# Expert sort ahead of the first row tables, and those tables behind the first half of the first expert products

## The reference

```python
p_grp = softmax(t @ w_grp); g_sel = argmax(p_grp); g_w = max(p_grp)
le_g = (t @ w_exp) of the 8 experts of group g_sel
top_v, top_i = top_k(softmax(le_g), 2); top_v /= sum(top_v)
combine = g_w * one_hot(g_sel) * within          # (tokens, 32 experts)
hid = einsum('nd,edf->nef', t, w_ein)            # 1024 -> 2 x 256 for each expert
a, b = split(hid, 2)
act = silu(a) * b * combine
out = einsum('nef,efd->nd', act, w_eout)         # 256 -> 1024
```

## Time and profile before

| | us |
|---|---|
| median of 3 runs (lowest, highest) | 753.07 (752.62, 753.54) |
| the profiled execution's own time | 755.45 |
| its span, first to last instruction | 753.8 |
| TensorE busy | 696.9 (92%) |
| TensorE weight loads busy | 398.8 (53%) |
| VectorE busy | 278.3 (37%) |
| ScalarE busy | 172.0 (23%) |
| GpSimd busy | 84.5 (11%) |

### The profile page before, as it was taken

One profiled execution on the slowest core, in us unless ns is written; L12 is line 12 of the kernel. 1 busy time (PEld: TensorE's weight loads), 2 busy tenths in 40 slices (PEclk: granted clock), 3 DMA queues, 4 the chain that ended last, 5 costly groups with the idle time before them and its releaser, 6 DMA issues.

```text
span 753.8 us, 13479 instructions
## 1 busy us (share of the span) xinstructions
PE 696.9 (92%) x5136; PEld 398.8 (53%) x5136; DVE 278.3 (37%) x886; ACT 172.0 (23%) x410; POOL 84.5 (11%) x127
## 2 busy tenths in 40 slices
PE   5899899999999999799998999999999997888894
PEld 2687577558776665454555776664333332222342
DVE  2553123610102787664530322485411211111256
ACT  0223344112102564322242001331110101010102
POOL 0201000002500343110000000001212121112000
PEclk9999999999999999999999999999999999999998
DMA  8999997717344963899999992438999999999981
GB/s 239 383 411 396 410 366 236 309 68 276 113 157 180 359 256 120 313 363 389 392 378 385 420 407 87 191 104 312 419 418 418 418 419 417 419 419 418 420 254 72
DMA packets 63273, 236.15 MB, mean 313 GB/s; under 512 B 9733, under 2 KB 20878, under 8 KB 48293
## 3 DMA queue, kind: packets, MB, share of 16 engines
q1 hardware_dynamic: 52884, 218.73, 74.9%
q0 software_dynamic: 6432, 14.74, 5.3%
q10 hardware_dynamic: 3888, 1.77, 0.9%
HBM read 230.52 MB, written 19.14 MB: 331 GB/s over the span
## 4 chain that ended last, share of the span: by engine, by line
PE 62%; DMA 16%; SPq 13%; DVE 4%; issue 3%; ACTq 1%; ACT 1%; POOL 0%; POOLq 0%; DVEq 0%
PE bank L628 12%; SPq L485 7%; PE bank L1159 5%; PE bank L1038 5%; PE bank L1022 5%; SPq L504 4%; DMA arena<-in_w_eout 4%; DMA arena<-in_w_in 4%; PE bank L672 3%; PE bank L747 2%; PE bank L1186 2%; PE bank L565 2%; PE bank L970 2%; DMA arena<-h_rows,rows_of_slots_in 2%; PE bank L884 2%
## 5 line engine op out<-in xcount | busy, mean ns | idle before, releaser
L1159 PE MATMUL bank<-arena 128*32 128x512 f32 (+1 forms) x896 | 110.9, 610 | 14.2 <-DMA arena<-in_w_ein 14.0
L628 PE MATMUL bank<-arena 128*128 128x320 f32 x384 | 107.6, 439 | 2.8 <-DMA arena<-in_w_in 2.8
L628 PEld LDWEIGHTS bank<-arena 128*128 128x128 f32 x384 | 72.9, 191 | 34.7 <-DMA arena<-in_w_in 3.1
L1159 PEld LDWEIGHTS bank<-arena 128*32 128x32 f32 (+1 forms) x896 | 31.2, 114 | 82.9 <-issue 77.6
L1186 PE MATMUL bank<-arena 128*32 128x512 f32 (+1 forms) x464 | 58.3, 595 | 4.5 <-DMA arena<-in_w_eout 4.1
L2035 DVE COPY arena<-bank 128x512 f32<-128x512 f32 x14 | 9.7, 692 | 108.0 <-PE bank L1117 108.0
L1488 ACT ACTIVATE arena<-bank 128x256 f32<-128x256 f32 x16 | 6.2, 386 | 149.9 <-PE bank L1159 146.9
L1312 ACT ACTIVATE arena<-bank 32x320 f32<-32x320 f32 x60 | 25.8, 430 | 45.5 <-PE bank L628 45.0
L1038 PE MATMUL bank<-arena 128*128 128x320 f32 x128 | 35.0, 432 | 0.0
L1022 PE MATMUL bank<-arena 128*128 128x320 f32 x128 | 34.8, 432 | 0.0
L1186 PEld LDWEIGHTS bank<-arena 128*32 128x32 f32 (+1 forms) x464 | 15.6, 112 | 36.2 <-issue 29.8
(11 more groups left out here) (413 smaller groups left out, 1011.5 us busy)
## 6 DMA issues: line engine op xcount, KB each, us to landing
arena<-in_w_ein SPq DMA_DIRECT2D x52, 1024.0 KB, 25.2
arena<-in_w_eout SPq DMA_DIRECT2D x26, 1024.0 KB, 26.9
arena<-in_w_ada SPq DMA_DIRECT2D x12, 2048.0 KB, 14.3
arena<-in_w_in SPq DMA_DIRECT2D x10, 2048.0 KB, 10.4
arena<-in_k_pages SPq DMA_DIRECT2D x64, 320.0 KB, 6.0
arena<-in_v_pages SPq DMA_DIRECT2D x64, 320.0 KB, 9.2
arena<-in_w_ein SPq DMA_DIRECT2D x3, 4096.0 KB, 21.8
arena<-in_w_eout SPq DMA_DIRECT2D x3, 2048.0 KB, 13.1
```

The lines of the kernel that those rows point to most:

```text
L628: m = mm(banks[c % 4][:, 0:N], ring[q][:, k, P * (c % 4):P * (c % 4 + 1)], hT[:, k, :], start=(k == 0), stop=(k == KD - 1))
L1159: m = mm(banks[2 + p % 2][r:r + n, :], xeT[p % 2][:, k, r:r + n], wi2[p % 3][:, e, k, :], start=(k == 0), stop=(k == KD - 1))
```

## The change

On VectorE, the sort of the experts by count moves ahead of the first table's inputs. On SP, the issue of pair 3's input weights moves ahead of the load of pair 4's two expert numbers. On TensorE, the first table's product moves behind the first half of pair 0's products, and the first half of pair 1's turn moves behind the second half of those products. No instruction is added or removed.

```diff
@@ -506,8 +506,8 @@
 
             sp.wait_ge(s_ord, 1)
             this = sorted_pair(3)
+            sorted_in(3, this)
             after = sorted_pair(4)
-            sorted_in(3, this)
             for p in range(3, LAST - 1):
                 sorted_in(p + 1, after)
                 sorted_out(p, this)
@@ -1095,12 +1095,6 @@
                 te.wait_ge(s_hr, 1 + t)
                 m = first_rows(t, 0)
             m.then_inc(s_hh, 1)
-            te.wait_ge(s_m, 6)
-            te.wait_ge(s_hr, 8)
-            for j in range(8):
-                m = mm(banks[3][:, 0:3], first_hit[0:RT, j, :], first_hitv[0:RT, j, :], start=(j == 0), stop=(j == 7))
-            m.then_inc(s_tab, 1)
-
             def all_tables():
                 te.wait_ge(s_m, 7)
                 for j in range(8):
@@ -1190,12 +1184,17 @@
             te.wait_ge(s_wi[0], 16)
             te.wait_ge(s_xtA, 1)
             first_hidden(0).then_inc(s_hh, 1)
+            te.wait_ge(s_m, 6)
+            te.wait_ge(s_hr, 8)
+            for j in range(8):
+                m = mm(banks[3][:, 0:3], first_hit[0:RT, j, :], first_hitv[0:RT, j, :], start=(j == 0), stop=(j == 7))
+            m.then_inc(s_tab, 1)
             for t in range(4):
                 m = first_rows(t, 1)
             m.then_inc(s_xt, 1)
-            turn_rows(1, (0,))
             te.wait_ge(s_xtD, 1)
             first_hidden(1).then_inc(s_hd, 1)
+            turn_rows(1, (0,))
             turn_rows(1, (1,))
             for p in range(1, LAST):
                 hidden(p)
@@ -2093,6 +2092,21 @@
             for t in range(4):
                 ve.scalar_tensor_tensor(first_slots[R, t], slots_here, rowE[R, 4 + t:5 + t], first_slots[R, t], ALU.is_equal, ALU.add)\
                     .then_inc(s_m, 1)
+            every = [RT, FREE_E, FREE_E]
+            beaten = ranked[R]
+            link(ve.scalar_tensor_tensor(key[R], cnt[R], float(E), cst[R, C_E:C_E + E], ALU.mult, ALU.subtract))
+            link(ve.tensor_tensor(beaten, key[R, FIXED:E].unsqueeze(1).to_broadcast(every),
+                                  key[R, FIXED:E].unsqueeze(2).to_broadcast(every), ALU.is_gt))
+            link(ve.tensor_reduce(rank[R], beaten, AX, ALU.add))
+
+            same = ranked[0:1]
+            wide1 = [1, FREE_E, FREE_E]
+            link(ve.tensor_tensor(same, cst[0:1, C_E:C_E + FREE_E].unsqueeze(2).to_broadcast(wide1),
+                                  rank[0:1].unsqueeze(1).to_broadcast(wide1), ALU.is_equal))
+            link(ve.tensor_tensor(same, same, cst[0:1, C_E + FIXED:C_E + E].unsqueeze(1).to_broadcast(wide1), ALU.mult))
+            link(ve.tensor_reduce(key[0:1, 0:FREE_E], same, AX, ALU.add))
+            ve.tensor_copy(order[:, :], key[0:1, 0:FREE_E]).then_inc(s_ord, 1)
+
             link(ve.tensor_copy(index[:, :], rowE[R]))
             slot_of()
             places(first_hit, 0, 8)
@@ -2101,21 +2115,6 @@
             token4 = cst[R, C_TOK:C_TOK + 4].unsqueeze(2).to_broadcast([RT, 4, 3])
             ve.tensor_tensor(first_hitv[R, 0:4], first_hitv[R, 0:4], token4, ALU.mult)
             ve.tensor_tensor(first_hitv[R, 4:8], first_hitv[R, 4:8], token4, ALU.mult).then_inc(s_m, 1)
-
-            every = [RT, FREE_E, FREE_E]
-            beaten = ranked[R]
-            link(ve.scalar_tensor_tensor(key[R], cnt[R], float(E), cst[R, C_E:C_E + E], ALU.mult, ALU.subtract))
-            link(ve.tensor_tensor(beaten, key[R, FIXED:E].unsqueeze(1).to_broadcast(every),
-                                  key[R, FIXED:E].unsqueeze(2).to_broadcast(every), ALU.is_gt))
-            link(ve.tensor_reduce(rank[R], beaten, AX, ALU.add))
-
-            same = ranked[0:1]
-            wide1 = [1, FREE_E, FREE_E]
-            link(ve.tensor_tensor(same, cst[0:1, C_E:C_E + FREE_E].unsqueeze(2).to_broadcast(wide1),
-                                  rank[0:1].unsqueeze(1).to_broadcast(wide1), ALU.is_equal))
-            link(ve.tensor_tensor(same, same, cst[0:1, C_E + FIXED:C_E + E].unsqueeze(1).to_broadcast(wide1), ALU.mult))
-            link(ve.tensor_reduce(key[0:1, 0:FREE_E], same, AX, ALU.add))
-            ve.tensor_copy(order[:, :], key[0:1, 0:FREE_E]).then_inc(s_ord, 1)
 
             ve.wait_ge(s_tab, 1)
             link(ve.tensor_scalar(gone, banks[3][:, 0:3], 0.5, NOWHERE, ALU.is_le, ALU.mult))
```

More of the change, by code:

```diff
@@ L2095, in _ @@
                     .then_inc(s_m, 1)
[L2096 to L2103, removed]
             every = [RT, FREE_E, FREE_E]
@@ L2118, in _ @@
             ve.tensor_copy(order[:, :], key[0:1, 0:FREE_E]).then_inc(s_ord, 1)
+            link(ve.tensor_copy(index[:, :], rowE[R]))
+            slot_of()
+            places(first_hit, 0, 8)
+            link(ve.tensor_tensor(first_hitv[R], cst[R, C_ROW:C_ROW + 3].unsqueeze(1).to_broadcast([RT, 8, 3]),
+                                  high[R].unsqueeze(2).to_broadcast([RT, 8, 3]), ALU.is_equal))
+            token4 = cst[R, C_TOK:C_TOK + 4].unsqueeze(2).to_broadcast([RT, 4, 3])
+            ve.tensor_tensor(first_hitv[R, 0:4], first_hitv[R, 0:4], token4, ALU.mult)
+            ve.tensor_tensor(first_hitv[R, 4:8], first_hitv[R, 4:8], token4, ALU.mult).then_inc(s_m, 1)
             ve.wait_ge(s_tab, 1)
```

## The result

| | us |
|---|---|
| before, median of 6 runs (lowest, highest) | 753.37 (752.62, 754.65) |
| changed, median of 6 runs (lowest, highest) | 760.86 (758.52, 762.44) |
| ratio, 95% interval | 1.0096 [1.0075, 1.0116] |
| profiled execution of the changed kernel, its span | 759.82, 758.1 |

The change makes the kernel 7.5 us slower. The forecast was 1.2 us slower, in a range that ended at 755.7. In all ratios of this document, executions over 1.5% above the fastest of their kernel count as slow and are left out: two of e3, one of e5 (2477.81 us) and one of the kernel before.

What follows compares the result with a forecast made beforehand. The end was taken as set by a gapless weight stream that begins when `hidden(1)` ends. New waits less the old gather wait made `hidden(1)` +1.25 us later, passed on whole: 753.07 to 754.3, range 752.7 to 755.7.

Steps and rivals of the forecast that it cites:

- the rows' second half follows to 511.14: TensorE behind the tables, which end at 507.30: the second half of pair 0's rows takes 3.84 us, as before.
- The order's own part: TensorE up to `hidden(1)`: new idle times less the old gather wait start it later, taken as +1.25 us.
- all its waits: TensorE's new idle times: 0.67 ahead of first products, 0.49 of tables, 0.68 of second products, 0.09 of `hidden(1)`.
- The rival "absorbed": TensorE waits for weights later, so a late `hidden(1)` doesn't matter and the time stays 753.1; 8 in 100.
- The earlier weights: Rival: pair 3's weights, issued 2.9 us earlier, bring the stream's end forward, to 750.2; 8 in 100.
- SP's two later loads: Pair 4's two number loads fall into SP's 7.6 us wait behind pair 3's second half; cost zero, uncovered 1.30.
- the nearest row: Pair 2's gather before, 4.4 us beside weights with 2.5 us overlap; taken for pair 1's gather, hidden by 2.1 us.
- alone: Pair 1's gather in the kernel before, read as having the DMA engines to itself: 3.8 us.
- the 6.3 us of pair 3's first half: Time from issue to landing of these weights, used to put 2.5 us of overlap on each of two gathers.
- The price of a late gather: Rival: pair 1's gather takes 9.9 us beside weights, the first turn waits for it; +4.65 us, 757.7; 10 in 100.

Runs made afterwards that it cites:

- e3: The kernel before with SP's part of the change alone (pair 3's issue ahead of the load of pair 4's numbers); ratio to before 1.0043.
- e5: The changed kernel with its three waits filled by unused products and a full product behind each of the first seven table products; ratio to before 1.0043.
- e4: The kernel before, with first-half input weights from pair 4 on issued once half the row chunks of the buffer's previous pair are multiplied; ratio 0.9966.
- e7: The changed kernel with SP's order as before, pair 4's numbers loaded ahead of pair 3's issue; ratio to before 1.0086.
- e10: The kernel before with VectorE's part of the change alone, the sort moved ahead; ratio to before 1.0094.
- e2: The kernel before with TensorE's part of the change alone, VectorE and SP as before; ratio to before 1.0038.
- e1: The changed kernel with TensorE's three new waits filled by 3, 2 and 3 products into an unused bank; ratio to before 1.0030.
- e9: The changed kernel with a full product behind each of the first seven thin table products, waits left idle; ratio to before 1.0022.
- e6: The kernel before with the table product done twice, nothing moved; ratio to before 1.0035.

## Why the prediction was wrong

**The step that failed** is the durations behind the tables: "the rows' second half follows to 511.14" at 3.84 us and the second products at 3.58, taken from a stretch of before in which the clock is full throughout, for a stretch with other work ahead. The clock had no term, no bound and no rival. Measured: 6.97 and 6.60 us, 6.15 of the 7.49 us.

**What stood.** The order's own part was foretold as +1.25 and is 7.49 - 6.15 = 1.34; the profile after has all its waits, in place and nearly in size. That a late `hidden(1)` moves the end by as much, and that no room absorbs it, held: +7.49 there, +7.63 at pair 13's weights, 7.5 in the medians. e4 shows it from the other side, though it frees the halves of all later pairs early too. The rival "absorbed" is out.

**The earlier weights** did nothing that shows (e7), as argued. Pair 3 was issued at 502.04, 8.45 us behind the first row products against 11.12 before; this only lengthened the gap ahead of its own second half, which waits for the second products. SP's two later loads stayed hidden.

**The gather** took more than the 4.4 us of the nearest row. DMA issues of the changed kernel, to landing last:

```profile
arena<-h_rows,rows_of_slots_in POOLq DMA_INDIRECT x1, 5.9
```

Started at 505.71, it landed at 511.6, ahead of the turn at 518.3. With the clock full, the turn would have come 6.15 us sooner, at 512.15: still in time, but by some 0.6 us and not by 2.1. Two readings were off here. The 3.8 us that the prediction calls "alone" belong to a gather with the weights issued 1.1 us behind it; in e10, where none were issued until 5 us later, it took 3.5. And the 6.3 us of pair 3's first half are a median of two pieces, of which the first took 5.3; the second was still in flight at the 514.3 that was taken for the end. The price of a late gather was real, as e3 shows at 8.5. The Trainium skill (DMA: Bandwidth & Descriptors, Queues, rings and completion order) has the engines take turns between queues; the gathers here took 3.5 us alone, 4.4 and 5.9 where 2 MB of weights had been issued 3.9 and 3.7 us ahead, 8.1 in e2, where they were issued 0.6 us ahead, and 8.5 where both were issued together. That the weights slow a gather agrees. That in e3 the gather, the smaller of the two, lands at 512.7, as late as the last of the weights (two pieces from 504.28 on, 5.2 us for the first, a median of 6.5), is not what equal turns let one expect.

**What caused the fall** is shown as far as this: TensorE's new order, with the thin products in their new place, is enough for it (e2); the profile with filled waits still has it (e1); it doesn't appear in the profiles in which full products stand between the thin ones, waits or not (e9, e5); and weights in flight are neither needed (e6, e10) nor enough for it (e9). The Trainium skill (TensorE: Matmul & The Clock Gate, Part 1) says that the clock follows how busy the array has been of late, and warns of idle gaps. The traces agree in e10 and e3, where the clock fell in gaps of 4.7 and 5.4 us; they add that it can fall with no idle time in TensorE's rows, as in e1, where eight thin products and then row products stood ahead of the fall.

Not settled: why the fall lasted 13.7 us in one execution of the changed kernel, 10.2 in another, 6.8 with the waits filled. The old place has full products straight behind the tables, the new one row products and a wait; e6 fell for 3.4 us in the old place. No run kept the new place and changed only what follows, so the part that the row products have in the fall is open as well.

## What to carry to other kernels

A duration read from a trace holds with the work that stood ahead of it. When small products are moved on TensorE, read the granted clock around their new place and give a fall to half clock a price: what ran behind it here took 1.8 times its time until the clock came back. Mixing thin products with full ones, even useless ones, can be cheaper than leaving them in a row, as in e9. And before weights are issued earlier, ask what else the DMA engines carry then: a gather on the critical path may pay for it.

## What the runs showed of the hardware

The granted clock went to half while TensorE's busy share was 1.00 and no idle time stood in its timeline (e1, 505 to 512 us). A full busy share did not mean that the clock held.
